# First head of stick breaking prepared during the value projection

## The reference, cut to what matters

```python
proj = h @ w_in[l]
sb_q, sb_k, sb_v, gq, gk, gv, gg, gf = jnp.split(proj, offsets, axis=-1)
...
z = jnp.einsum('bhqd,bhkd->bhqk', qb, kb).astype(jnp.float32) * scale
mask = s_pos[None, :] < t_pos[:, None]
log_one_minus = jnp.where(mask, jax.nn.log_sigmoid(-z), 0.0)
...
between = lax.cumsum(shifted, axis=3, reverse=True)
weights = jnp.where(mask, jnp.exp(jax.nn.log_sigmoid(z) + between), 0.0)
outs.append(jnp.einsum('bhqk,bhkd->bhqd', weights.astype(vb.dtype), vb))
```

## Time and profile before

| what | us |
|---|---|
| median of 3 runs (lowest, highest) | 3302.2 (3300.24, 3306.65) |
| the profiled execution, its own time | 3302.0 |
| its span | 3300.3 |
| PE busy in the span | 2938.9 |
| DVE, ACT, POOL busy | 1851.4, 1027.9, 908.1 |

### The profile page before, as it was taken

How to read it: one execution, slowest core, us unless ns; L and a number is a source line. 1 busy time by engine, 2 the same in 40 slices (tenths; PEclk the granted TensorE clock), 3 DMA queues, 4 the chain that set the end, 5 groups by cost and what they waited for, 6 DMA issues and landing times. The chain is left out here.

```text
span 3300.3 us, 40638 instructions
## 1 busy us (share of the span) xinstructions
PE 2938.9 (89%) x15957; PEld 2526.1 (77%) x15957; DVE 1851.4 (56%) x2924; ACT 1027.9 (31%) x1466; POOL 908.1 (28%) x304
## 2 busy tenths in 40 slices
PE   4969998799999999979677678889999899999996
PEld 3869897687888888867556676789779688888885
DVE  7617764665454545562589877865336533333336
ACT  5424544222222222231456455633222111111111
POOL 1212331113233233340122512211121233333333
PEclk9989998799999999989788789999999999999998
DMA  6733333401111111101223322230102111111111
GB/s 225 264 103 72 72 76 125 164 16 72 40 50 46 56 51 38 64 26 62 67 83 124 92 63 60 63 116 28 43 20 71 64 51 41 48 51 51 51 51 51
DMA packets 112339, 240.06 MB, mean 73 GB/s; under 512 B 53524, under 2 KB 72471, under 8 KB 99015
## 3 DMA queue, kind: packets, MB, share of 16 engines
q1 hardware_dynamic: 107175, 220.70, 20.6%
q10 hardware_dynamic: 4320, 14.29, 1.3%
q0 software_dynamic: 704, 3.15, 0.3%
HBM read 202.58 MB, written 38.67 MB: 73 GB/s over the span
## 5 line engine op out<-in xcount | busy, mean ns | idle before, releaser
L1020 PE MATMUL psum<-h_hi,w_hl 128*128 128x512 f32 x2432 | 751.3, 390 | 16.8 <-DVE ffn_relu L1597 12.8
L1009 POOL TENSOR_TENSOR w_hl<-w_raw,w_hl 128x2048 fp32r<-128x2048 f32 x65 | 324.0, 4984 | 862.9 <-ACT w_hl L1003 862.9
L1020 PEld LDWEIGHTS psum<-h_hi,w_hl 128*128 128x128 f32 x2432 | 456.7, 188 | 113.7 <-issue 18.4
L1037 PE MATMUL psum<-w_hl,ffn_a_hi 128*128 128x512 f32 x1600 | 494.1, 390 | 6.5 <-DVE residual L1360 6.5
L1020 PE MATMUL psum<-h_lo,w_hl 128*128 128x512 f32 x1216 | 473.8, 390 | 0.0
L450 PE MATMUL psum<-w_hl,h_hi 128*128 128x256 f32 (+1 forms) x1920 | 353.8, 287 | 29.9 <-POOL w_hl L413 15.1
L1037 PEld LDWEIGHTS psum<-w_hl,ffn_a_hi 128*128 128x128 f32 x1600 | 301.3, 188 | 69.5 <-DVE residual L1360 6.9
L1003 ACT ACTIVATE w_hl<-w_raw 128x2048 fp32r<-128x2048 f32 x65 | 124.6, 1916 | 692.4 <-PE psum L1037 355.0
L413 POOL TENSOR_TENSOR w_hl<-w_raw,w_hl 128x2048 fp32r<-128x2048 f32 (+1 forms) x39 | 181.8, 4662 | 552.6 <-ACT w_hl L405 552.6
L450 PEld LDWEIGHTS psum<-w_hl,h_hi 128*128 128x128 f32 x1920 | 305.3, 196 | 31.7 <-issue 16.0
L1037 PE MATMUL psum<-w_hl,ffn_a_lo 128*128 128x512 f32 x800 | 311.9, 390 | 0.0
(11 more groups left out here) (375 smaller groups left out, 5078.7 us busy)
## 6 DMA issues: line engine op xcount, KB each, us to landing
w_raw<-in_w_up SPq DMA_DIRECT2D x38, 1024.0 KB, 4.8
w_raw<-in_w_down SPq DMA_DIRECT2D x27, 1024.0 KB, 4.9
ada_w<-in_w_ada ACTq DMA_DIRECT2D x26, 512.0 KB, 4.6
w_raw<-in_w_in_T SPq DMA_DIRECT2D x12, 1024.0 KB, 7.0
ada_w<-in_w_ada SPq DMA_DIRECT2D x22, 512.0 KB, 5.3
w_raw<-in_xa_wkv SPq DMA_DIRECT2D x8, 1024.0 KB, 5.4
w_raw<-in_w_in_G SPq DMA_DIRECT2D x8, 648.0 KB, 5.4
p1G<-sb_stage SPq DMA_DIRECT2D x16, 324.0 KB, 3.6
```

Of the source, the lines that this page charges most:

```text
L1009: pool.tensor_tensor(self.k.w_lo[s][:, :], self.k.w_raw[s][:, :], self.k.w_hi[s][:, :].bitcast(F), ALU.subtract).then_inc(self.k.wsem["w_r ...
L1020: m = pe.matmul(k.bank[b][:, :], w[:, t * CW + f * P:t * CW + (f + 1) * P], h[:, t, half * 512:half * 512 + 512], start=t == 0 and w is w_ ...
L1037: m = pe.matmul(k.bank[4 + out % 4][:, :], a[f][:, tile * P:(tile + 1) * P], w[:, f * D + half * 512:f * D + half * 512 + 512], start=f == ...
```

## The change

A new class `FirstStick` owns the tiles of head 0 (k, k high and low, q, q split) and the two masks, at a fixed address (`STICK_AT`). `project("in1V")` calls it: SP issues its four loads first of all, ACT rounds k and q behind its two roundings of weights, POOL makes the masks ahead of its splits, and splits k and q behind them. The same block now does for `lin_G` (`then`): load of chunks 0 and 1, rounding and splitting of chunk 0. `stick_breaking` takes the tiles over and leaves these steps out. Its counts shift: `made` counts only the two fills of `rest`, and ACT waits for both of them before its first Sigmoid; PE doesn't wait for `made`; `his` and `los` start with head 1; `loaded[0]` counts from head 2. The tile `q` is now used from head 1 on, so head 1's load waits for no subtraction.

```diff
@@ -47,6 +47,7 @@
 MEM, MEM_HEADS, MEM_HD = 256, 4, 256
 BAND = 384
 KEPT_AT = 229248
+STICK_AT = 211968
 
 
 class Kernel:
@@ -489,7 +490,53 @@
         self.chunks(pe, step)
 
 
-def project(k, name, lin, dst, bias=None, ahead=None, mods=None, turns=None, mod_rows=None, mod_stored=None):
+class FirstStick:
+
+
+    def __init__(self, k, at, qkT):
+        self.qkT = qkT
+        self.kk, self.k_hi, self.q_split, self.q = (
+            k.over(f"stick_{n}", [P, S], R if n in ("k_hi", "q_split") else F, at + 4 * S * j)
+            for j, n in enumerate(("k", "k_hi", "q_split", "q")))
+        self.k_lo = k.over("stick_k_lo", [P, S], R, at)
+        self.limit, self.unit = (k.over(f"stick_{n}", [P, P], BF, at + 16 * S + 2 * P * j)
+                                 for j, n in enumerate(("limit", "unit")))
+        self.loaded, self.his, self.los, self.made = (k.sem("stick_" + n) for n in ("loaded", "his", "los", "made"))
+
+    def load(self, sp):
+        for r in range(2):
+            half = slice(r * HD, (r + 1) * HD)
+            sp.dma_start(self.kk[half, :], self.qkT[SB_HEADS * HD:(SB_HEADS + 1) * HD, :]).then_inc(self.loaded, 16)
+            sp.dma_start(self.q[half, :], self.qkT[0:HD, :]).then_inc(self.loaded, 16)
+
+    def round(self, act):
+        act.wait_ge(self.loaded, 64)
+        act.activation(self.k_hi[:, :], self.kk[:, :], ACT.Copy).then_inc(self.his, 1)
+        act.activation(self.q_split[:, :], self.q[:, :], ACT.Copy).then_inc(self.his, 1)
+
+    def masks(self, pool):
+        pool.memset(self.limit[:, :], 0.0).then_inc(self.made, 1)
+        pool.memset(self.unit[:, :], 0.0).then_inc(self.made, 1)
+        pool.wait_ge(self.made, 2)
+        pool.affine_select(out=self.limit[:, :], in_=self.limit[:, :], compare_op=ALU.is_gt, fill=NEG, base=0,
+                           pattern=[[-1, P]], channel_multiplier=1).then_inc(self.made, 1)
+        pool.affine_select(out=self.unit[:, :], in_=self.unit[:, :], compare_op=ALU.not_equal, fill=1.0, base=0,
+                           pattern=[[-1, P]], channel_multiplier=1).then_inc(self.made, 1)
+        pool.wait_ge(self.made, 4)
+
+    def split(self, pool):
+        pool.wait_ge(self.his, 1)
+        pool.tensor_tensor(self.k_lo[:, :], self.kk[:, :], self.k_hi[:, :].bitcast(F), ALU.subtract)\
+            .then_inc(self.los, 1)
+        pool.wait_ge(self.los, 1)
+        pool.wait_ge(self.his, 2)
+        pool.tensor_tensor(self.q_split[HD:P, :], self.q[HD:P, :], self.q_split[HD:P, :].bitcast(F),
+                           ALU.subtract).then_inc(self.los, 1)
+        pool.wait_ge(self.los, 2)
+
+
+def project(k, name, lin, dst, bias=None, ahead=None, mods=None, turns=None, mod_rows=None, mod_stored=None,
+            stick=None, then=None):
 
 
 
@@ -508,6 +555,8 @@
             def _(sp):
                 if bias is not None:
                     sp.dma_start(bt[:, :], bias if kind == "T" else rows(bias)).then_inc(bias_in, 16)
+                if stick is not None:
+                    stick.load(sp)
 
                 def store(c, i, s):
                     sp.wait_ge(*lin.at("lin_evac", s, 4 * i + 4))
@@ -531,6 +580,8 @@
                     looped(sp, pairs - 1, ahead_by_two)
                 if n % 2:
                     lin.load(sp, n - 1, n // 2, s0)
+                if then is not None:
+                    then.early(sp, "load", 2)
                 for s in range(2 if pairs else 0):
                     store(2 * pairs - 2 + s, pairs - 1, s ^ s0)
                 if ahead:
@@ -554,6 +605,8 @@
                     return
                 for ch in range(min(2, n)):
                     lin.hi(act, ch, ch // 2, ch % 2 ^ lin.s0)
+                if stick is not None:
+                    stick.round(act)
                 for ch in range(n):
                     if ch + 2 < n:
                         lin.hi(act, ch + 2, ch // 2 + 1, ch % 2 ^ lin.s0)
@@ -566,12 +619,20 @@
                 if mod_rows is not None:
                     act.wait_ge(mod_mm, 1)
                     act.activation(mods.turned_rows[:, :], k.bank[4 * lin.s0][0:4 * KT, 0:P], ACT.Copy).then_inc(mod_out, 1)
+                if then is not None:
+                    then.early(act, "hi", 1)
 
             @block.gpsimd
             def _(pool):
+                if stick is not None:
+                    stick.masks(pool)
                 lin.split_lo(pool)
+                if stick is not None:
+                    stick.split(pool)
                 if ahead:
                     ahead.early(pool, "lo", 1)
+                if then is not None:
+                    then.early(pool, "lo", 1)
 
             @block.tensor
             def _(pe):
@@ -1690,7 +1751,7 @@
         e.wait_ge(sem, value)
 
 
-def stick_breaking(k, qkT, v, mix, lin, lin_dst, mod_stored):
+def stick_breaking(k, qkT, v, mix, lin, lin_dst, mod_stored, first):
 
 
 
@@ -1703,21 +1764,18 @@
     with ExitStack() as c:
         sem = lambda n: k.sem("sb_" + n)
         q = k.sb(c, "sb_q", [P, S])
-        q_split = [k.sb(c, f"sb_q_split{s}", [P, S], R) for s in range(2)]
-        kk, k_lo = [], []
-        for s in range(2):
-            at = nc.sbuf_base
-            kk.append(k.sb(c, f"sb_k{s}", [P, S]))
-            k_lo.append(k.over(f"sb_k_lo{s}", [P, S], R, at))
-        k_hi = [k.sb(c, f"sb_k_hi{s}", [P, S], R) for s in range(2)]
+        q_split = [first.q_split, k.sb(c, "sb_q_split1", [P, S], R)]
+        at = nc.sbuf_base
+        kk = [first.kk, k.sb(c, "sb_k1", [P, S])]
+        k_lo = [first.k_lo, k.over("sb_k_lo1", [P, S], R, at)]
+        k_hi = [first.k_hi, k.sb(c, "sb_k_hi1", [P, S], R)]
         LW = lin.width
         vv = [k.w_raw[s][:, KT * LW:KT * LW + NT * HD].rearrange("p (i d) -> p i d", d=HD) for s in range(2)]
         rest = [k.sb(c, f"sb_rest{s}", [P, S + 1]) for s in range(2)]
         wgt = [k.sb(c, f"sb_wgt{s}", [P, S]) for s in range(2)]
         wT = [k.sb(c, f"sb_wT{s}", [P, NT, P]) for s in range(2)]
         o = [k.over(f"sb_o{s}", [P, NT, HD], F, k.w_hl_offset(s, 0, KT * LW)) for s in range(2)]
-        limit = k.sb(c, "sb_limit", [P, P], BF)
-        unit = k.sb(c, "sb_unit", [P, P], BF)
+        limit, unit = first.limit, first.unit
         stage = [k.over(f"sb_stage{s}", [P, NT // 2, LW], F, k.w_hl_offset(s, 1, KT * LW)) for s in range(2)]
         lin_stored = [sem(f"lin_stored{s}") for s in range(2)]
         hi_lo = sem("hi_lo")
@@ -1741,7 +1799,7 @@
                     for r in range(2):
                         sp.dma_start(kk[s][r * HD:(r + 1) * HD, :],
                                      qkT[(SB_HEADS + h) * HD:(SB_HEADS + h + 1) * HD, :]).then_inc(loaded[s], 16)
-                    reached(sp, los, 2 * h - 1)
+                    reached(sp, los, 2 * h - 3)
                     for r in range(2):
                         sp.dma_start(q[r * HD:(r + 1) * HD, :], qkT[h * HD:(h + 1) * HD, :]).then_inc(loaded[s], 16)
 
@@ -1760,7 +1818,6 @@
                     sp.dma_start(lin_dst[half * 512:half * 512 + 512, h * LW:(h + 1) * LW]
                                  .rearrange("(i p) n -> p i n", p=P), stage[half][:, :, :])\
                       .then_inc(lin_stored[half], 16)
-                load(0)
                 lin.load(sp, 0, 0, slot(0))
                 load_v(0)
                 load_v(1)
@@ -1784,30 +1841,20 @@
                 def split_qk(n):
                     h, s = n // NT, n // NT % 2
                     if n % NT == 0:
-                        pool.wait_ge(his, 2 * h + 1)
-                        if h:
-                            pool.wait_ge(*lin.at("w_ready", slot(h - 1), (h - 1) // 2 + 1))
+                        pool.wait_ge(his, 2 * h - 1)
+                        pool.wait_ge(*lin.at("w_ready", slot(h - 1), (h - 1) // 2 + 1))
                         pool.tensor_tensor(q_split[s][HD:P, :], q[HD:P, :], q_split[s][HD:P, :].bitcast(F),
                                            ALU.subtract).then_inc(los, 1)
-                        pool.wait_ge(los, 2 * h + 1)
-                        pool.wait_ge(his, 2 * h + 2)
+                        pool.wait_ge(los, 2 * h - 1)
+                        pool.wait_ge(his, 2 * h)
                         pool.tensor_tensor(k_lo[s][:, :], kk[s][:, :], k_hi[s][:, :].bitcast(F),
                                            ALU.subtract).then_inc(los, 1)
-                pool.memset(limit[:, :], 0.0).then_inc(made, 1)
-                pool.memset(unit[:, :], 0.0).then_inc(made, 1)
                 for s in range(2):
                     pool.memset(rest[s][:, :], 1.0).then_inc(made, 1)
-                pool.wait_ge(made, 4)
-                pool.affine_select(out=limit[:, :], in_=limit[:, :], compare_op=ALU.is_gt, fill=NEG, base=0,
-                                   pattern=[[-1, P]], channel_multiplier=1).then_inc(made, 1)
-                pool.affine_select(out=unit[:, :], in_=unit[:, :], compare_op=ALU.not_equal, fill=1.0, base=0,
```

(21 more changed lines are left out.)

## The result

The edit is faster: 3291.57 us against 3302.24, a ratio of 0.9965 with a 95% interval of 0.9955 to 0.9975 (6 runs each). Forecast were 3290.9 and a range of 3284.5 to 3296.5. The profiled execution took 3290.22 us, with a span of 3288.5; against the one of before (3302.0 and 3300.3) that is 11.8 less. The interval lies clear of 1, so the gain is not noise.

What follows compares the result with a forecast made beforehand. PE, busy 89% of the span, bounds the kernel; time can be won where it idles or runs at half clock. Gains of 10.6 + 0.3 + 0.4 = 11.3 us gave 3290.9 us, range 3284.5 to 3296.5.

Steps and rivals of the forecast that it cites:

- The gap: PE's idle time between value projection and first scores: 6.4 to 6.7 us stay of 19.4, for evacuation, store and barrier.
- the 0 of my sum for the added work: Value projection: the loads, roundings, splits and masks moved there are covered and cost 0.
- The first Sigmoid: Attention's start on ScalarE: at 232.4 instead of 243.00, behind the fills and then the table load; gain 10.6 us.
- The price of the load: Sigmoid table load ahead of the first Sigmoid: 1.3 us from its start to the ACTIVATE, not the skill's 2.66.
- The ramp: First Sigmoid to first inner tile: without GpSimd's split beside VectorE, gain 0.3 us, bounds 0 and 1.5.
- The clock: PE's half clock around the first inner tile: gain 0.4 us, between 1.05 and nothing, the two likeliest cases.
- (c): Rival, attention stage: the clock falls more often, one or two falls more give 3294.3 to 3297.7; chance 0.14.
- (d): Rival, attention stage: the clock falls less often, one fewer gives 3287.5, none at all 3282.4; chance 0.12.
- v: Head 0's values, issued first: landing at 234.6 to 236.4, wanted at 236.2 to 236.5; 0, up to 0.2 lost.
- Handed on whole: GLA and everything behind it starts behind a barrier, so the whole gain, 11.3 us, reaches the end.

Runs made afterwards that it cites:

- e10: The edit with rounding and split of k and q put ahead of those of the second value weights: 3300.49 us (one run).
- e1: The edit with only head 0's k, q and masks moved, inner weights prepared at the attention's start as before: 3290.95 us (5 runs), ratio 0.9962.
- e2: The kernel before with only the inner weights' load, rounding and split moved, k, q and masks left: 3302.32 us, ratio 1.0.
- c: The edit itself, unchanged, run once more: 3289.99 us (5 runs), ratio 0.9956 to the kernel before.
- e1b: The kernel of e1 run once more, unchanged: 3296.26 us (6 runs), ratio 0.9966 to the kernel before.
- e5: The edit with short fills of rest, only columns read before they are written; table load left where it is: 3284.29 us (one run).
- e6: The edit with the Sigmoid table loaded first on ScalarE and short fills of rest: 3290.2 us (5 runs), ratio 0.9961.
- e3: The edit with SP issuing k and q of head 1 ahead of v of heads 0 and 1: 3294.42 us (10 runs), ratio 0.998.
- e4: The edit with the Sigmoid table loaded at the start of ScalarE's list, fills left whole: 3289.76 us (one run).
- e7: The edit with 44 unread 128x256 matmuls filling PE's idle time behind the last value product: 3287.03 us (one run).

## Why the prediction was right

*The gap.* Right: 6.54 us stay of 19.43, forecast 6.4 to 6.7. No engine waits for what was added to the value projection: the gap is as long, and PE has no idle time between its first and last value product in any trace. e10 shows the cover by itself, and e1 and e2 show that both halves of the edit were needed. But the products end at 222.80 + 0.28, 0.33 later than before, after a start 1.1 us earlier, with 3.4 us more at half clock there. I had not counted on either. From first to last value product PE takes 47.40 us before, 47.81 in e2, and 47.38 (c) to 48.82 (e1b) in the twelve traces in which k and q are prepared there, 48.3 in the mean. So the 0 of my sum for the added work may hide some 0.9 us of lower clock. With one trace of before this stays open.

*The first Sigmoid.* The sum had a gain of 10.6, the trace has 11.21 (243.00 to 231.79). Counted from the block's start I had 3.3 us, and it took 2.21. The step that was off is where the table load stands. I put it behind both waits, at 231.1. It stood behind PE's scores only and ran beside the fills (e5: taking the fills away changes nothing). The price of the load was right: 1.29 us from its start to the Sigmoid in the edit, 1.30 in e2 and e5. The Trainium skill ("ScalarE: Activation LUTs", What ACT_TABLE_LOAD costs) has 2.66 us for load and drain. The traces here don't agree: where nothing else was waited for, 1.29 to 1.30 us pass. The block's start at 229.58 instead of 229.12 took 0.46 back.

*The ramp.* Forecast 0.3, measured 0.78 (5.80 to 5.02 us from Sigmoid to tile). I had taken the one wait of PE for DVE that the earlier trace rows show, 0.28 us; there was a second one, of 0.25 us, at the first transposes. DVE and PE in order of time, before and then in the edit:

```profile
244.05 0.78 DVE L1922 TENSOR_TENSOR sb_wgt<-sb_wgt,sb_rest 128x128 f32<-128x128 f32 x1
244.88 0.47 PE L1844 MATMUL psum<-ident,sb_wgt 128*128 128x128 f32 x1 [0.25 <-DVE sb_wgt L1922]
```

```profile
232.56 0.29 DVE L1966 TENSOR_TENSOR sb_wgt<-sb_wgt,sb_rest 128x128 f32<-128x128 f32 x1
232.77 0.68 DVE L1963 TENSOR_TENSOR_SCAN sb_rest<-sb_rest 128x256 f32<-128x256 f32 x1
```

All of the 0.78 lies at these two transposes. The third scores begin 0.50 us after the first Sigmoid in both kernels; the first transposes follow 1.38 us behind them before and 0.93 in the edit, the next ones 1.75 and 1.43 us behind the first. Both times PE had waited for DVE, whose instructions up to there were longer beside GpSimd's split: first scan 0.70 us against 0.42, first multiplication 0.78 against 0.29, second scan 1.36 against 0.68. e2, where the split is also gone but the start is not earlier, has a ramp of 5.01, so it is the split that counts and not the start. Nor is it that PE has two steps' scores ready: in e6 it is still at the second step's when the first Sigmoid starts, and the ramp is 5.01 as well. e1, where the split is still there (3.52 us from 235.00), has 5.53: its first multiplication (0.79) and second scan (1.36) are as long as before, its first scan (0.43) is not. Why that one is short beside the split is not shown.

*The clock.* Forecast 0.4, between a clock that comes back as long after the restart and one that does so as long after the tile. In the trace it came back at 237.9, 8.3 us after the restart and 1.1 after the tile. At the scores behind the first tile the gain is 13.36 us (253.60 to 240.24), 1.4 more than at the tile. In c it came back at 235.1, 6.5 after the restart and half a us before the tile. At the first change of a head the clock then fell for over 6 us. Windows of the edit:

```profile
255.00:261.00 6.00, 6.00 (x30) 6.00 (x29) 4.42 (x6) 0.92 (x2) 5.28 (x4) 0.51 0.53 169
256.00:528.00 272.00, 261.04 (x1997) 249.70 (x1996) 185.89 (x294) 123.10 (x188) 78.78 (x40) 0.97 0.29 69
```

and the gain went down to 11.8 there (DVE's copy at 272.08 before, at 260.30 after). The mean over the stage is 0.97, that of before: the falls move, their sum stays. Rivals (c) and (d) were the right kind of uncertainty, and in this trace they cancelled.

*v.* Right, and for the reason given: first in the queue, it was not late (e3 prices it at 3.3 us where it is). I had let it land 5.5 us after issue or later, it took 3.0 to 4.7.

*Handed on whole.* Nearly. GLA starts 13.8 us earlier (545.81 to 531.98), the span is 11.8 shorter. Across the traces the time behind GLA's start lies between 2754.2 and 2766.1 us, with no difference in code; 2 us are well within that. What moves it I have not isolated. The one trace of before, with 2754.5, is among the three shortest of the fourteen, so it also stays open whether a part of the gain is regularly lost behind GLA's start.

So the median was met to 0.7 us. The profiled execution gained 11.8 us where the sum had 11.3: errors of +1.1 (table load), +0.5 (ramp), +1.0 (clock) and +0.5 (the rest of the stage) against -0.5 (a later start) and -2.0 (behind GLA's start). The mechanism was right: the last wait ahead of the first Sigmoid set the gain. That the number is so close is in good part luck: the terms' errors cancelled, and the second set of runs, c, gave 14.1 us (3304.05 to 3289.99) where the first gave 10.7.

## What to carry to other kernels

At the start of a stage, look on every engine of the chain for the last wait ahead of its first instruction there. Moving one of two prerequisites can be worth nothing (e2) or a part (e1), and the pair more than the sum. A step that costs nothing because it runs during a wait, as the table load did before, can become the next wait when the step ahead of it is taken out. Where single runs spread over 10 us, compare points of the trace counted from the block's own start, and distrust a median of five runs.

## What the runs showed of the hardware that I had not expected

- In these traces it is not enough for a hidden table load that ACT is idle. With one wait directly ahead of the ACTIVATE the load ran before it (239.29). With two it ran behind the one that is written last, PE's scores (230.50, with ACT idle for 17 us; 242.89 in e2), but not behind the first: in the edit the fills ended only at 231.42. An explicit load at the start of the list ran at once (229.35 in e4). Why it falls this way is not shown.
- In e7, PE kept busy at full clock up to 1.28 us before the block's first scores didn't keep the clock up: granted 1.00 over 226 to 230, 0.53 over 230 to 236.8, in which PE was shown busy 5.38 of 6.80 us.
- v, 256 KB in rows of 256 bytes, landed in 3.0 to 4.7 us when it was issued first, against 6.7 to 7.3 for the same loads behind other traffic before.
